# Half-column level products, and a last feed-forward chunk worked by thirds of the tokens

## What is computed

```python
x1 = layer_norm(ALPHA * x + merged @ w_o, ln1_g, ln1_b)
up = x1 @ w_up                                   # 2816 value columns, 2816 gate columns
ext = jnp.concatenate([conv_prev.astype(up.dtype), up], axis=1)
conv = conv_b + sum(conv_w[j] * ext[:, j:j + T] for j in range(CONV_W))      # CONV_W = 3
val, gate = jnp.split(conv, 2, axis=-1)
ffn = (val * jax.nn.gelu(gate)) @ w_down
x2 = layer_norm(ALPHA * x1 + ffn, ln2_g, ln2_b)
e = (p @ w_pl) * jax.nn.sigmoid(x2 @ w_plg)
y = layer_norm(ALPHA * x2 + e, ln3_g, ln3_b)
```

## Time and profile before

| | us |
|---|---|
| median of 3 runs | 2348.92 (2347.63 to 2351.49) |
| profiled execution, its own time | 2349.89 |
| its span, first to last instruction | 2348.2 |
| TensorE busy | 2288.3, 97% |
| VectorE, ScalarE, GpSimd busy | 1280.9, 675.3, 269.1 |
| mean granted TensorE clock | 0.993 of full speed |

### The profile page before, as it was taken

The page is one execution under the profiler, slowest core; times in us unless marked ns, Lnnn a source line. Parts: engine busy times, 40 slices in busy tenths (PEclk is TensorE's granted clock), DMA queues, the critical chain, the costliest instruction groups (busy, mean ns, idle before and its releaser), DMA issues.

```text
span 2348.2 us, 31921 instructions
## 1 busy us (share of the span) xinstructions
PE 2288.3 (97%) x13055; PEld 2116.7 (90%) x13055; DVE 1280.9 (55%) x1696; ACT 675.3 (29%) x1100; POOL 269.1 (11%) x462
## 2 busy tenths in 40 slices
PE   8999999999999999999999999999999999999897
PEld 8997777898989899999998899999999999999686
DVE  2226753363636363112433666667676766767885
ACT  3124663333333332123221231222212122221310
POOL 0001222001010101000031210000000000000331
PEclk9999999999999999999999999999999999999998
DMA  5109654112120212213215011111101111111310
GB/s 159 42 24 253 165 153 127 52 28 85 29 84 21 86 28 79 80 46 104 59 63 170 1 46 46 37 45 36 54 27 54 45 36 45 36 45 35 115 52 36
DMA packets 154750, 160.27 MB, mean 68 GB/s; under 512 B 14538, under 2 KB 127158, under 8 KB 153990
## 3 DMA queue, kind: packets, MB, share of 16 engines
q1 hardware_dynamic: 145638, 128.91, 18.5%
q0 software_dynamic: 9008, 29.87, 4.0%
HBM read 122.27 MB, written 23.84 MB: 62 GB/s over the span
## 4 chain that ended last, share of the span: by engine, by line
PE 91%; DVE 3%; SPq 2%; issue 1%; ACT 1%; DMA 1%; POOL 0%; DVEq 0%; ACTq 0%; POOLq 0%
PE ps L613 73%; PE ps L1140 4%; PE ps L1019 3%; PE ps L930 2%; PE ps L793 1%; DVE sb L1645 1%; SPq L2572 1%; PE ps L645 1%; PE ps L775 1%; PE ps L753 1%; DVE sb L1749 0%; PE ps L981 0%; PE ps L776 0%; PE ps L960 0%; DMA kc<-k_lo 0%
## 5 line engine op out<-in xcount | busy, mean ns | idle before, releaser
L613 PE MATMUL ps<-x_hi,up_hi 128*128 128x384 f32 x1056 | 353.8, 335 | 0.1
L613 PE MATMUL ps<-x_hi,up_lo 128*128 128x384 f32 x1056 | 353.7, 335 | 0.0
L613 PE MATMUL ps<-x_lo,up_hi 128*128 128x384 f32 x1056 | 353.2, 334 | 0.0
L1194 ACT ACTIVATE sb<-ps 128x384 f32<-128x384 f32 (+5 forms) x332 | 132.5, 427 | 716.7 <-PE ps L613 664.2
L613 PE MATMUL ps<-x_hi,ring_hi 128*128 128x384 f32 x960 | 328.2, 342 | 3.4 <-DVE x_lo L1669 2.6
L613 PE MATMUL ps<-x_hi,ring_lo 128*128 128x384 f32 x960 | 322.4, 336 | 0.0
L613 PE MATMUL ps<-x_lo,ring_hi 128*128 128x384 f32 x960 | 322.4, 336 | 0.0
L2134 DVE TENSOR_TENSOR sb<-sb,ps 128x512 f32<-128x512 f32 x378 | 258.5, 688 | 114.1 <-PE ps L613 113.7
L613 PEld LDWEIGHTS ps<-x_hi,up_hi 128*128 128x128 f32 x1056 | 198.2, 188 | 2.7 <-DVE sb L1645 0.3
L613 PEld LDWEIGHTS ps<-x_lo,up_hi 128*128 128x128 f32 x1056 | 198.2, 188 | 2.4
L613 PEld LDWEIGHTS ps<-x_hi,up_lo 128*128 128x128 f32 x1056 | 198.2, 188 | 0.0
(11 more groups left out here) (280 smaller groups left out, 4243.3 us busy)
## 6 DMA issues: line engine op xcount, KB each, us to landing
ring_raw<-in_w_in SPq DMA_DIRECT2D x50, 512.0 KB, 3.9
up_raw<-in_w_up SPq DMA_DIRECT2D x44, 512.0 KB, 3.9
sb<-in_x_prompt SPq DMA_DIRECT2D x24, 512.0 KB, 8.3
down_raw<-in_w_down SPq DMA_DIRECT2D x22, 512.0 KB, 4.5
branch_b<-sb POOLq DMA_DIRECT2D x4, 1152.0 KB, 7.2
ob_raw<-branch_b POOLq DMA_DIRECT2D x3, 1536.0 KB, 7.4
kk<-k_hi SPq DMA_DIRECT2D x16, 256.0 KB, 4.3
sb<-in_cache_fox_k SPq DMA_DIRECT2D x8, 512.0 KB, 6.7
```

Of the source, the lines that this page charges most:

```text
L613: m = mm(out, l, r, start=(n == 0), stop=(n == len(pairs) - 1))
L1194: return act.activation(out, in_, ACT.Copy, scale=scale)
```

## The change

**Level products.** For levels 0 to 6 the moving operand is only the second half of each block (`second_halves`), 64 columns instead of 128; the stationary operand stays 128x128. The masked copy then takes 512 (and 64) columns instead of 1024 (and 128) and writes them to every block's second half in AT (`later_take`).

**Last chunk.** The up products of chunk 21 come third by third, both halves of a third together, and taps, gelu, product and h's two parts are made for a third at a time (`last_chunk`, `last_thirds`, `convolve_third`, `h_third`, `h_lo_third`). The down products of tiles 0 to 2 are worked as six half tiles in the chunk's banks around the last up product, and the statistics of tiles 0 and 1 are taken before the last third's taps. `last_down(3)` and `turn_x2(0)` stand ahead of `embed_p(2)`. The first two `row_rstd` move into the chunk, in front of the gathering of columns; of the calls that followed, one stays between GpSimd's `plg_lo(3)` and `plg_lo(4)`, and it is now the third. ScalarE's `plg_hi(0)`, which stood between the gelu and h_hi, and `keep_p(0)` stand behind the chunk now. SP loads ln2's gain and bias ahead of the slices of w_plg and those of ln3 behind them.

```diff
-            n = 6 * d + 3 * v + g
+            n = 6 * d + (2 * g + v if d == NC_FF - 1 else 3 * v + g)
...
+        Y_THIRDS = [(0, THIRD), (THIRD, 2 * THIRD), (2 * THIRD, 1168)]
...
+        def second_halves(a, l):
+
+            return a.rearrange("p (b a j) -> p b a j", a=2, j=HALVES[l])[:, :, 1, :]
...
+                def later(a, t, l):
+                    return second_halves(a[:, t], l) if l < 7 else a[:, t]
...
+                    w = 64 if l < 7 else P
...
-                        m = mm(o[:, t], a[:, t], c[:, t], start=True, stop=True)
+                        m = mm(o[:, n * w:(n + 1) * w], a[:, t], later(c, t, l), start=True, stop=True)
...
-                        mm(o[:, 0:P], a[:, SEQ:T], c[:, SEQ:T], start=True, stop=True)\
+                        mm(o[:, 0:w], a[:, SEQ:T], later(c, slice(SEQ, T), l), start=True, stop=True)\
...
+            def last_chunk():
+                up(0, LAST, 0, 0)
+                up(0, LAST, 1, 0)
+                up(0, LAST, 0, 1)
+                new_columns(0, LAST - 1)
+                down(0, LAST - 1, DOWN_AFTER[2])
+                up(0, LAST, 1, 1)
+                down(0, LAST - 1, DOWN_AFTER[3])
+                up(0, LAST, 0, 2)
+                down(0, LAST - 1, DOWN_AFTER[4])
+                turn_p_early()
+                down(0, LAST, range(4))
+                up(0, LAST, 1, 2)
+                down(0, LAST, range(4, 6))
...
+                pe.wait_ge(s_hl, LAST + n // 3 + 1)
...
             pe.wait_ge(cn_free, LAST)
+            last_down(3)
+            turn_x2(0)
             embed_p(2)
             pe.wait_ge(s_cg, 2 * LAST + 4)
             o = take(pe, "columns")
             for v in range(2):
                 m = tr(o[0:18, v * P:(v + 1) * P], cn[:, v, :], ident)
             m.then_inc(filled("columns"), 1)
-            pe.wait_ge(s_hl, NC_FF)
-            pe.wait_ge(s_dl, NC_FF)
-            for n in range(4):
-                last_down(n)
-            turn_x2(0)
...
+            def last_thirds():
+                for g in range(3):
+                    for v in range(2):
...
+                        if (g, v) == (0, 1):
+                            act.wait_ge(s_wdi[LAST % 2], 16 * (LAST // 2 + 1))
+                            copy(wdh[:, LAST % 2, :], rawd[:, LAST % 2, :]).then_inc(s_dh, 1)
+                            act.wait_ge(s_ple, 16)
+                            for k in range(2):
+                                copy(plh[:, k, :], rpl[:, k, :]).then_inc(s_plh, 1)
+                        if (g, v) == (1, 0):
+                            new_columns(0, LAST - 1)
+                        if (g, v) == (2, 0):
+                            o = product(act, "pTs")
+                            copy(pTh, o[:, 0:768].rearrange("p (n k t) -> p n k t", n=3, k=2)).then_inc(s_x2h, 1)
+                    a, b = Y_THIRDS[g]
+                    act.wait_ge(s_conv, 2 * LAST + 2 * g + 2)
+                    act.activation(y[:, 1, a:b], y[:, 1, a:b], ACT.Gelu_apprx_tanh).then_inc(s_gel, 1)
+                    act.wait_ge(s_hm, LAST + g + 1)
...
+            keep_p(0)
+            plg_hi(0)
+            keep_p(1)
+            plg_hi(1)
             x2_hi(0)
-            plg_hi(KT - 1)
+            keep_p(2)
+            plg_hi(2)
+            act.wait_ge(s_ocn, 32 * LAST)
+            o = product(act, "columns")
+            copy(cno, o[0:18, 0:256]).then_inc(drained("columns"), 1)
+            for k in range(3, KT):
+                plg_hi(k)
...
+                def later_take(l, last):
+
+                    hf = HALVES[l]
+                    nb = 64 // hf
+                    mask = second_halves(levm[:, l * P:(l + 1) * P], l)
+                    if last:
+                        v, n, o = AT[:, SEQ:T], 1, product(dve, ("lv", h, l, 1))
+                    else:
+                        v, n, o = AT[:, 0:SEQ], NP, product(dve, ("lv", h, l, 0))
+                    v = v.rearrange("p (n b a j) -> p n b a j", b=nb, a=2, j=hf)[:, :, :, 1, :]
+                    mask = mask.rearrange("p (n b) j -> p n b j", n=1).to_broadcast([P, n, nb, hf])
+                    return dve.copy_predicated(v, mask, o[:, 0:n * 64].rearrange("p (n b j) -> p n b j", b=nb, j=hf))
...
+            def convolve_third(v, g):
+
+                n, (a, b) = 2 * LAST + 2 * g + v + 1, Y_THIRDS[g]
+                i, m = up_use(0, LAST, v, g)
+                dve.wait_ge(up_free[i], m + 1)
...
+                dve.tensor_scalar(yv, u[:, a:b], w[0], w[3], ALU.mult, ALU.add).then_inc(s_cv1, 1)
+                dve.wait_ge(s_cv1, n)
+                stt(yv, u[:, a + 1:b + 1], w[1], yv, ALU.mult, ALU.add).then_inc(s_cv2, 1)
+                dve.wait_ge(s_cv2, n)
+                stt(yv, u[:, a + 2:b + 2], w[2], yv, ALU.mult, ALU.add).then_inc(s_conv, 1)
+
+            def h_third(g):
+                a, b = Y_THIRDS[g]
+                dve.wait_ge(s_gel, LAST + g + 1)
+                dve.tensor_tensor(y[:, 0, a:b], y[:, 0, a:b], y[:, 1, a:b], ALU.mult).then_inc(s_hm, 1)
...
+            def last_thirds():
+                dve.wait_ge(s_hl, LAST)
+                convolve_third(0, 0)
+                convolve_third(1, 0)
+                add_down(0, LAST - 1, DOWN_AFTER[2])
+                h_third(0)
+                dve.wait_ge(s_dh, LAST + 1)
+                dve.tensor_tensor(wdl[:, LAST % 2, :], rawd[:, LAST % 2, :], wdh[:, LAST % 2, :].bitcast(F32), ALU.subtract)\
+                    .then_inc(s_dl, 1)
+                h_lo_third(0)
+                for k in range(2):
+                    dve.wait_ge(s_plh, k + 1)
+                    dve.tensor_tensor(pll[:, k, :], rpl[:, k, :], plh[:, k, :].bitcast(F32), ALU.subtract).then_inc(s_pl, 1)
+                convolve_third(0, 1)
+                convolve_third(1, 1)
+                add_down(0, LAST - 1, DOWN_AFTER[3])
+                h_third(1)
+                h_lo_third(1)
+                add_down(0, LAST - 1, DOWN_AFTER[4])
+                dve.wait_ge(s_x2h, 1)
+                o = product(dve, "pTs")
+                dve.tensor_tensor(pTl, o[:, 0:768].rearrange("p (n k t) -> p n k t", n=3, k=2), pTh.bitcast(F32),
+                                  ALU.subtract).then_inc(drained("pTs"), 1)
+                add_down(0, LAST, range(4))
+                for n in range(2):
+                    tile_added(n)
+                    second_i[n] = stats_of(x1[:, n, :])
+                add_down(0, LAST, range(4, 6))
+                convolve_third(0, 2)
+                convolve_third(1, 2)
...
+            dve.wait_ge(s_g1, 64)
+            centre(x1[:, 0, :], second_i[0], g2)
+            h_third(2)
+            second_b(0)
+            h_lo_third(2)
+            plg_lo(0)
+            add_last(3)
+            centre(x1[:, 1, :], second_i[1], g2)
             plg_lo(1)
-            add_last(0)
-            dve.wait_ge(s_g1, 96)
-            second_a(0)
-            add_last(1)
-            second_b(0)
-            second_a(1)
-            add_last(2)
-            add_last(3)
+            second_b(1)
             x2_lo(0)
-            second_b(1)
-            plg_lo(KT - 1)
             add_last(4)
             add_last(5)
+            plg_lo(KT - 1)
+            dve.wait_ge(s_const, 48)
             for n in range(NT - 1):
...
+                pool.wait_ge(s_conv, 4 * j + 2 * d + v + 1 + (4 if d == LAST else 0))
...
@@ -2467,6 +2607,9 @@
                 cached(j, d, 1)
                 if d:
                     store_new(j, d - 1)
+                if d == LAST:
+                    row_rstd()
+                    row_rstd()
                 gather(j, d, 0)
                 gather(j, d, 1)
...
             plg_lo(2)
+            copied(pool, "columns")
+            store_new(0, LAST, columns_copied=True)
             plg_lo(3)
             row_rstd()
-            copied(pool, "columns")
-            store_new(0, LAST, columns_copied=True)
             plg_lo(4)
-            row_rstd()
             plg_lo(5)
             plg_lo(6)
-            for n in range(2 * NT - 2):
+            for n in range(2 * NT - 3):
                 row_rstd()
             for i in range(3):
...
                 sp.wait_ge(up_full[b], 6 * NC_FF // 4)
+            bcast(ln2_g[0], g2, s_g1)
+            bcast(ln2_b[0], b2, s_g1)
             for k in range(KT):
                 sp.dma_start(rplg[:, k, :], w_plg[0, k * P:(k + 1) * P, :]).then_inc(s_xt[k], 16)
-                if k == 1:
-                    for v, dst in ((ln2_g, g2), (ln2_b, b2), (ln3_g, g3), (ln3_b, b3)):
-                        bcast(v[0], dst, s_g1)
+            bcast(ln3_g[0], g3, s_const)
+            bcast(ln3_b[0], b3, s_const)
```

More of the change, by code:

```diff
@@ L2181, in stats_of, with halves_or_last @@
+            def halves_or_last(j, d):
+                if d == LAST:
+                    last_thirds()
+                else:
+                    halves(j, d)
             def stats_of(z):
```

117 lines of the change are left out of this document (67 added, 50 removed).

## The result

| | before | after |
|---|---|---|
| median of five runs each | 2351.49 us (2347.63 to 2352.91) | 2359.63 us (2358.54 to 2363.11) |
| profiled execution, its span | 2349.89, 2348.2 | 2363.11, 2361.4 |

What follows compares the result with a forecast made beforehand. TensorE, busy 97% of the 2348.2 us span, was taken as the bound. 2349.89 - 5.8 (levels) + 6.3 (last chunk and gate) = 2350.4, less 1.0 for the profiled run's excess over the median: 2349.4 us, range 2344.5 to 2355.

Steps and rivals of the forecast that it cites:

- The level term: Linear attention's level products: 480 instructions on half the columns save 0.012 us each, 5.8 us in all.
- the narrowest fp32 product ... 0.100 us: Sample heads' turn, 16 moving columns: 0.70 / 7 = 0.100 us a matmul, taken as the level products' new pitch.
- 64 columns want 0.058 us: Level products: at 0.456 ns a column and two passes, 64 moving columns need 0.058 us, well under 0.100.
- rival 1: Level products save nothing because a 128x128 fp32 weight load holds 0.112 us; time 2355.2 us, chance 0.13.
- the start-to-start stays above 0.110: Level products: the sign, in us between matmul starts, that would decide for the weight load holding the pitch.
- my 2.4 us: Level products: the saving by the skill's 107 ns weight-load rule, 480 x 0.005 us, instead of 5.8 us.
- The tail: Last chunk and gate: gate products end 5.0 us later, plus 1.3 us of slow clock, together +6.3 us.
- the stall: Last chunk: the fourth down product waits from 2159.3 to 2162.3 for VectorE's adds, costing TensorE 3.0 us.
- rival 4: Last chunk: thirds cost more, through a clock lowered by the stall or slower short taps; 2351 to 2356 us, chance 0.15.
- The slow clock at the end of the gate: Gate: TensorE, mostly waiting from 2204 to 2215, then runs on a slow clock, put at 1.3 us.
- The lower bound of +1.8: Last chunk and gate: cost in us if row_rstd does not hold GpSimd, whose five subtractions alone end at 2212.1.
- The mechanism of the tail: Last chunk and gate: TensorE stalls, then the gate waits for slices that GpSimd delays behind row_rstd and tile 2's statistics.

Runs made afterwards that it cites:

- e1: The kernel before with only the level products on 64 columns and matching masked copies: 2349.16 us against 2349.22, ratio 0.9997.
- e4: The kernel before with level products on 64 moving columns and only their first 64 weight columns, leaving work out: 2329.76 us against 2349.22.
- e6: The changed kernel with GpSimd's third row_rstd moved behind slice 6: 2353.13 us, against 2349.43 for the kernel before, ratio 1.0014.
- e7: The changed kernel with the second third's taps moved behind the adds that free banks: 2356.17 us, against 2349.43 for the kernel before, ratio 1.0027.
- e2: The changed kernel with level products back on 128 columns, leaving only the thirds: 2359.81 us, against 2349.22 for the kernel before, ratio 1.0040.

## Why the prediction was wrong

1. **The level term was mis-sized: -5.8 us forecast, 0 measured** (e1). The step that failed is "the narrowest fp32 product ... 0.100 us". It divided the length of a row of eight matmuls by seven, but the first of them is followed by the second after 0.02 us. Leave out the first two, and the matmuls (the first line) and the weight loads (the second), of which I had read no row, say the same:

```profile
432.01 0.82 PE L863 MATMUL ps<-sb 128*128 128x16 f32 x6
...
431.99 0.75 PEld L863 LDWEIGHTS ps<-sb 128*128 128x128 f32 x6
```

(0.82 - 0.26) / 5 and (0.75 - 0.19) / 5 are both 0.112 us with 16 moving columns, as with 128: the floor was the weight load, and 64 columns could not go below it. The other half of my argument, that 64 columns want 0.058 us, is true (e4). This was rival 1 at 0.13; its test, "the start-to-start stays above 0.110", reads 0.109 by the matmuls' row ((1.90 - 0.27) / 15, with the same early second start) and 0.112 by the loads, so the test named the wrong row too. The Trainium skill's rule in "TensorE: Matmul & The Clock Gate", section "LDWEIGHTS (loading the stationary operand)", names the right mechanism, a time by columns; its 107 ns for 128 columns is 112 here, and my 2.4 us from it was the difference between its figure and 0.112, not a gain.

2. **The tail was mis-sized by 2.1 us in the profiled pair: +6.3 forecast, +8.4 measured.** In old times (after minus 4.74), with the forecast in brackets: restart behind the stall 2162.2 (2162.3); end of the last up product 2183.2 (2181.6); turn of x2 tile 0 at 2192.3 (2190.7); gate 2203.5 (2200.3); end of slice 3 at 2205.3 (2203.7); of slice 6 at 2216.8 (2215.3); turn of tile 1 at 2219.6 (2216.7 + 1.3). Three terms were too small.
   - **The clock was low behind the stall**, a mean of 0.91 in its stretch. The three down products behind it took 3.41 us (2166.90 to 2170.31) in place of 2.05, at 0.427 us a matmul where full clock gives 0.228, which is the lower of the clock's two levels (1.2 GHz); the up product behind them took 4.52 in place of 4.2. The turn of x2 tile 0 carries these 1.6 us on. That is the first half of rival 4, left out of the sum although I had counted the same effect behind the old gap of 7.72 us. GpSimd's slice 2 began only 0.5 us late, as I had put 1.0 us between its rounding and its start and the trace has 0.1.
   - **GpSimd's slice 2 took 3.44 us where I wrote 2.37**, because VectorE's scale of tile 1, a two-input step, had started 0.07 us ahead of it (2202.97); I had let VectorE wait for GpSimd and never the reverse.
   - **The slow clock at the end of the gate cost 2.0 us, not 1.3**: 1.35 in the last two products (2221.60 to 2224.32 in place of 1.37) and 0.7 in the turn behind them (1.46 us in place of 0.79).

   Two sums of mine were off without moving the forecast. The five VectorE steps ahead of the adds come to 7.95 us, not 7.8. The lower bound of +1.8 rests on subtractions that end at 2212.1; by my own durations they end at 2210.9, which gives +0.6. That e6, which tests this bound, has a tail of +1.8 over before is luck, since its stall and slow clock were not in the bound.

3. **The mechanism of the tail was right.** The stall, the starved gate, GpSimd's third row_rstd and its wait for tile 2's statistics are in the trace as written (2.85 us for 3.0, 5.61 for 6, 2.62 for 2 to 3); the turn of x2 tile 0 is 7.8 us nearer to the chunk's start where some 9 were forecast. e6 and e7 confirm them by taking the row_rstd and the stall away.

4. **The chances.** The two errors have the same sign. The cases were priced one at a time, rival 1 at 2355.2 and rival 4 at 2351 to 2356; both together, 2357 to 2362 by my own numbers, fell outside the range. The upper end should have held their sum. The two terms are 7.9 of the 10.2 us by which the median missed. The other 2.3 are not tied to one cause. By the medians of the larger samples the thirds cost 10.1 to 10.6 us (e2 among them), and part of the difference to 8.4 is that I priced them against a single trace, in which the old tail took its slower course (221.6 us against a mean of 220.6).

## What to carry over

When a matmul has weights of its own, read the weight loads' row beside the matmul's, and leave out the first start of a group: the larger side sets the pitch, and cutting one side alone gives nothing. Cutting both to what the mask keeps gave 7.0 us here. Before an operation is moved to an idle GpSimd, look whether VectorE has two-input steps there: eight slices on one engine, with the scale of tile 1 behind them, beat a split over two by 4.9 us. Price a stall of TensorE with the slow clock that may follow it, here 1.5 to 1.7 us behind 2.85 of waiting in three traces (after, e2, e6). And when two engines reach for the same thing within 0.1 us, look at a second trace before you build on the first.
